# Decay factors and scaled copies of a delta rule moved to ScalarE, a mask moved back, modulation spread over 18 tiles

## The reference

```
proj = h @ w_in;  qkv, z, b_raw, a_raw = split(proj)
qkv  = silu(causal_dwconv(qkv, conv_w))          # 4 taps
q, k = l2_normalize(q) * dk**-0.5, l2_normalize(k)
beta = sigmoid(b_raw);  g = -exp(a_log) * softplus(a_raw + dt_bias)
G    = cumsum(g);  decay = exp(G_i - G_j) for i >= j, else 0
L    = strict_lower((k*beta) @ k.T * decay);  A = L + I
u, w = A^-1 (v*beta),  A^-1 (k*beta*exp(G))
attn = (q @ k.T) * decay
per chunk: v_new = u - w @ S;  o = (q*exp(G)) @ S + attn @ v_new
           S = S*exp(g_last) + (k*exp(g_last - G)).T @ v_new
out  = rms_norm(o) * silu(z) @ w_out
```

## Time and profile before

| | us |
|---|---|
| three runs | 1538.74, 1539.1, 1534.84; median 1538.74 |
| profiled execution | 1539.63, its span 1537.8 |
| busy, TensorE | 1391.5 (90% of the span) |
| busy, VectorE | 851.6 (55%) |
| busy, ScalarE | 533.9 (35%) |
| busy, GpSimd | 171.3 (11%) |
| mean granted clock of TensorE | 0.952 |

### The profile page before, as it was taken

One profiled execution on the slowest core, in us unless ns is written; L12 is line 12 of the kernel. 1 busy time (PEld: TensorE's weight loads), 2 busy tenths in 40 slices (PEclk: granted clock), 3 DMA queues, 4 the chain that ended last, 5 costly groups with the idle time before them and its releaser, 6 DMA issues. The chain is left out here.

```text
span 1537.8 us, 17933 instructions
## 1 busy us (share of the span) xinstructions
PE 1391.5 (90%) x6983; PEld 1121.7 (73%) x6983; DVE 851.6 (55%) x1384; ACT 533.9 (35%) x956; POOL 171.3 (11%) x171
## 2 busy tenths in 40 slices
PE   5798889889879999999998696889989999999997
PEld 5676767779768878887886474646767888888885
DVE  4679899647454654555545538966453323332335
ACT  2353522445342222221223434557343222221321
POOL 0013230004310000000001101220010000000002
PEclk9899999899989999999999798889999999999999
DMA  9443412110404545554532120010102223322321
GB/s 330 142 164 111 162 56 83 56 55 1 164 28 155 201 139 189 185 196 166 167 121 69 33 71 28 28 56 2 55 28 82 82 82 110 110 82 82 110 73 65
DMA packets 102854, 158.36 MB, mean 103 GB/s; under 512 B 9326, under 2 KB 74107, under 8 KB 102779
## 3 DMA queue, kind: packets, MB, share of 16 engines
q1 hardware_dynamic: 91898, 115.40, 22.6%
q0 software_dynamic: 10880, 41.95, 7.8%
HBM read 155.24 MB, written 2.10 MB: 102 GB/s over the span
## 5 line engine op out<-in xcount | busy, mean ns | idle before, releaser
L396 PE MATMUL ps<-h_hi,w_hi 128*128 128x512 f32 x960 | 389.6, 406 | 6.4 <-DVE h_lo L824 6.4
L397 PE MATMUL ps<-h_lo,w_hi 128*128 128x512 f32 x960 | 382.7, 399 | 0.0
L398 PE MATMUL ps<-h_hi,w_lo 128*128 128x512 f32 x960 | 382.2, 398 | 0.0
L380 DVE TENSOR_TENSOR w_lo<-raw,w_hi 128x1024 fp32r<-128x1024 f32 x172 | 210.7, 1231 | 265.9 <-ACT w_hi L374 265.6
L374 ACT ACTIVATE w_hi<-raw 128x1024 fp32r<-128x1024 f32 x180 | 187.9, 1049 | 150.4 <-PE ps L1935 142.9
L396 PEld LDWEIGHTS ps<-h_hi,w_hi 128*128 128x128 f32 x960 | 183.9, 192 | 50.5 <-issue 9.0
L397 PEld LDWEIGHTS ps<-h_lo,w_hi 128*128 128x128 f32 x960 | 184.0, 192 | 43.2 <-issue 1.7
L398 PEld LDWEIGHTS ps<-h_hi,w_lo 128*128 128x128 f32 x960 | 183.2, 191 | 43.6
L448 DVE SCALAR_TENSOR_TENSOR ada_acc<-ada_in,c_act,ada_acc 128x512 f32<-128x512 f32 x147 | 112.8, 768 | 3.9
L1933 PE MATMUL ps<-w_hi,g_hi 128*128 128x512 f32 x256 | 101.6, 397 | 2.6 <-DVE w_lo L380 2.6
L1800 ACT ACTIVATE g_hi<-tmp 128x512 fp32r<-128x512 f32 x44 | 27.8, 632 | 211.9 <-DVE tmp L1835 211.9
(11 more groups left out here) (369 smaller groups left out, 2059.9 us busy)
## 6 DMA issues: line engine op xcount, KB each, us to landing
raw<-in_ffn_w_in_dram SPq DMA_DIRECT2D x44, 1024.0 KB, 5.1
ada_in<-in_ada_w_dram POOLq DMA_DIRECT2D x40, 1024.0 KB, 5.6
raw<-in_ffn_w_out_dram SPq DMA_DIRECT2D x20, 1024.0 KB, 5.0
raw<-in_gdn_w_in_dram SPq DMA_DIRECT2D x16, 1024.0 KB, 5.7
ada_in<-in_ada_w_dram SPq DMA_DIRECT2D x4, 1024.0 KB, 7.3
x_t<-in_x_dram SPq DMA_DIRECT2D x2, 2048.0 KB, 9.8
early_slab<-in_ada_w_dram SPq DMA_DIRECT2D x4, 1024.0 KB, 12.4
raw<-in_gdn_w_out_dram SPq DMA_DIRECT2D x4, 1024.0 KB, 5.0
```

Source lines behind the costliest of these rows:

```text
L380: ops.tensor_tensor(lo, raw_tile(s, kc) if src is None else src, f32(hi), ALU.subtract).then_inc(lo_done, 1)
L396: nc.tensor.matmul(out_, hi[:, k, :], r_hi[:, k, :], start=k == 0, stop=False)
L397: nc.tensor.matmul(out_, hi[:, k, :], r_lo[:, k, :], start=False, stop=False)
L398: last = nc.tensor.matmul(out_, lo[:, k, :], r_hi[:, k, :], start=False, stop=k == kc - 1)
```

## The change

`act_j` takes the place of `pool_j` and `act_eb` that of `pool_eb`, both with four 128x128 instructions per unit in place of one 128x512. `dve_d` is gone: `act_abs` reads the bank of the grow matmul itself, with the negated column sums `g_neg` as its bias, again in four pieces, and stands behind `act_conv_out` in the slot. kk, l, the diagonals, the v turns and va each come one slot later; the elimination is cut into five slots in place of six. `pool_eu` starts when `diagonals` is signalled. The modulation's slabs 4 to 9 take three slots each. In the states, the scaled keys lie in other memory, two small sums come later, and around the last units the late weight splits come ahead of the norm and gate.

```diff
@@ -211,2 +211,3 @@
         gexp = fixed("gexp", [P, 3, NB, H], at=ba_at)
+        g_neg = gdn("g_neg", [P, NB, H])
         k_r = gdn("k_r", [P, NB, H])
@@ -916,3 +917,3 @@
         sq_ring = [diag[:, :, :].rearrange("p a b -> p (a b)"), tmp[:, 2, :]]
-        kg_ring = [diag[:, :, :], tmp[:, 2, :].rearrange("p (h n) -> p h n", h=HG)]
+        kg_ring = [h_raw[:, HG * g:HG * g + HG, (NB - 1) * P:NB * P] for g in range(NG)]
         r_ring = [tmp[:, i, :].rearrange("p (h n) -> p h n", h=HG) for i in range(2)]
@@ -926,4 +927,4 @@
             if TO_GATES <= n < TO_QUERIES:
-                if n == TO_GATES:
-                    act.wait_ge(ada_used, 18)
+                if n % 4 == 0:
+                    act.wait_ge(ada_used, 17 + (n - TO_GATES) // 4)
                 nc.scalar.activation(z_t[:, n - TO_GATES, :], bank, ACT.Silu).then_inc(sem("gdn_out_of_ps"), 1)
@@ -1042,2 +1043,3 @@
                                      ps[:, 6, 0:2 * NB * H].rearrange("p (t a b) -> p t a b", t=2, a=NB)))
+            ch(nc.vector.tensor_scalar(g_neg[:, :, :], gsum[:, 0, :, :], -1.0, None, ALU.mult))
             tt(gsum[:, 2, :, :], gsum[:, 1, :, :], gsum[:, 0, :, :], ALU.subtract).then_inc(sem("g_sums_made"), 1)
@@ -1045,13 +1047,15 @@
 
-        def pool_j(pool, m):
+        def act_j(act, m):
 
             if m == 0:
-                pool.wait_ge(sem("small_made"), 1)
-            nc.gpsimd.tensor_tensor(unit(eu, m), over_heads(upto[:, :]), along(columns(gate, m)),
-                                    ALU.mult).then_inc(sem("j_made"), 1)
+                act.wait_ge(sem("small_made"), 1)
+                act.wait_ge(sem("consts"), 2)
+            for h in range(HG):
+                nc.scalar.activation(eu[:, 4 * m + h, :], upto[:, :], ACT.Identity, scale=column(gate, m, h))\
+                    .then_inc(sem("j_made"), 1)
 
         def pe_grow(pe, m):
-            pe.wait_ge(sem("j_made"), m + 1)
+            pe.wait_ge(sem("j_made"), 4 * m + 4)
             if m >= 2:
-                pe.wait_ge(sem("d_made"), m - 1)
+                pe.wait_ge(sem("abs_made"), 4 * (m - 1))
             nc.tensor.matmul(ps[:, 2 + m % 2, :], ones[:, :], flat(unit(eu, m)), start=True, stop=True)\
@@ -1059,10 +1063,10 @@
 
-        def dve_d(dve, m):
-            dve.wait_ge(sem("grow_mm"), m + 1)
-            tt(unit(eu, m), heads_of(2 + m % 2), along(columns(gsum[:, 0, :, :], m)), ALU.subtract)\
-                .then_inc(sem("d_made"), 1)
-
         def act_abs(act, m):
-            act.wait_ge(sem("d_made"), m + 1)
-            nc.scalar.activation(unit(eu, m), unit(eu, m), ACT.Abs).then_inc(sem("abs_made"), 1)
+
+            if m == 0:
+                act.wait_ge(sem("g_sums_made"), 1)
+            act.wait_ge(sem("grow_mm"), m + 1)
+            for h in range(HG):
+                nc.scalar.activation(eu[:, 4 * m + h, :], heads_of(2 + m % 2)[:, h, :], ACT.Abs,
+                                     bias=column(g_neg, m, h)).then_inc(sem("abs_made"), 1)
 
@@ -1073,3 +1077,3 @@
             for half_ in range(2):
-                act.wait_ge(sem("abs_made"), 4 * half_ + 4)
+                act.wait_ge(sem("abs_made"), 16 * half_ + 16)
                 part = eu[:, 16 * half_:16 * half_ + 16, :]
@@ -1108,12 +1112,13 @@
 
-        def pool_eb(pool, m):
+        def act_eb(act, m):
 
             if m == 0:
-                pool.wait_ge(sem("nb_made"), 1)
-            pool.wait_ge(sem("e_made"), 1 + m // 4)
-            nc.gpsimd.tensor_tensor(unit(lt, m), unit(eu, m), along(columns(nb_f, m)), ALU.mult)\
-                .then_inc(sem("eb_made"), 1)
+                act.wait_ge(sem("nb_made"), 1)
+            act.wait_ge(sem("e_made"), 1 + m // 4)
+            for h in range(HG):
+                nc.scalar.activation(lt[:, 4 * m + h, :], eu[:, 4 * m + h, :], ACT.Identity, scale=column(nb_f, m, h))\
+                    .then_inc(sem("eb_made"), 1)
 
         def pool_eu(pool, m):
-            pool.wait_ge(sem("e_made"), 1 + m // 4)
+            pool.wait_ge(sem("eb_made"), 4 * m + 4)
             nc.gpsimd.tensor_tensor(unit(eu, m), unit(eu, m), over_heads(upto[:, :]), ALU.mult)\
@@ -1127,3 +1132,3 @@
             else:
-                pe.wait_ge(sem("d_made"), 7 + m)
+                pe.wait_ge(sem("abs_made"), 4 * (7 + m))
             k = chunk(H, m)
@@ -1136,3 +1141,3 @@
             dve.wait_ge(sem("kk_mm"), m + 1)
-            dve.wait_ge(sem("eb_made"), m + 1)
+            dve.wait_ge(sem("eb_made"), 4 * m + 4)
             tt(unit(lt, m), heads_of(2 + m % 2), unit(lt, m), ALU.mult).then_inc(sem("l_made"), 1)
@@ -1177,3 +1182,3 @@
 
-            if steps[0] == 1:
+            if 1 in steps:
                 dve.wait_ge(sem("bt_cut"), 2)
@@ -1309,9 +1314,5 @@
 
-            if n < 6 or 8 <= n < 14:
-                j = 4 + n // 3 if n < 6 else 7 + (n - 8) // 3
-                at = n % 3 if n < 6 else (n - 8) % 3
-                out_and(j, ((0, 1), (2,), (3,))[at])
-            elif n < 16:
-                out_and(6 if n < 8 else 9, (0, 1) if n % 2 == 0 else (2, 3))
-            elif n == 17:
+            if n < 18:
+                out_and(4 + n // 3, ((0, 1), (2,), (3,))[n % 3])
+            elif n == 19:
                 dve_ada_out(dve, ch, 9)
@@ -1319,4 +1320,3 @@
 
-        ELIMINATE = {17: range(1, 5), 18: range(5, 9), 19: range(9, 13), 20: range(13, 17), 21: range(17, 24),
-                     22: range(24, 31)}
+        ELIMINATE = {18: range(1, 7), 19: range(7, 12), 20: range(12, 17), 21: range(17, 23), 22: range(23, 31)}
 
@@ -1329,5 +1329,2 @@
                 out_split_act(act, 0, Q_GDN_OUT, n % 4)
-            if 9 <= n < 13:
-                act_abs(act, 2 * (n - 9))
-                act_abs(act, 2 * (n - 9) + 1)
             if not TO_GATES <= n < TO_QUERIES:
@@ -1340,4 +1337,13 @@
                 act_gates(act)
+            if 6 <= n < 10:
+                act_j(act, 2 * (n - 6))
+                act_j(act, 2 * (n - 6) + 1)
+            if 9 <= n < 13:
+                act_abs(act, 2 * (n - 9))
+                act_abs(act, 2 * (n - 9) + 1)
             if n == 12:
                 act_decay(act)
+            if 13 <= n < 17:
+                act_eb(act, 2 * (n - 13))
+                act_eb(act, 2 * (n - 13) + 1)
             if n == 25:
@@ -1378,14 +1384,10 @@
                 dve_g_sums(dve, ch)
-            if 8 <= n < 12:
-                dve.wait_ge(sem("g_sums_made"), 1)
-                dve_d(dve, 2 * (n - 8))
-                dve_d(dve, 2 * (n - 8) + 1)
-            if 13 <= n < 17:
-                dve_l(dve, 2 * (n - 13))
-                dve_l(dve, 2 * (n - 13) + 1)
-            if n == 16:
+            if 14 <= n < 18:
+                dve_l(dve, 2 * (n - 14))
+                dve_l(dve, 2 * (n - 14) + 1)
+            if n == 17:
                 dve_diagonals(dve)
-            if 17 <= n < 21:
-                dve_va(dve, 2 * (n - 17))
-                dve_va(dve, 2 * (n - 17) + 1)
+            if 18 <= n < 22:
+                dve_va(dve, 2 * (n - 18))
+                dve_va(dve, 2 * (n - 18) + 1)
             if n in ELIMINATE:
@@ -1421,4 +1423,4 @@
                 pe_g_sums(pe)
-            if n in (3, 6, 8, 11, 14, 16):
-                pe_ada(pe, {3: 4, 6: 5, 8: 6, 11: 7, 14: 8, 16: 9}[n])
+            if n % 3 == 0 and 3 <= n < 19:
+                pe_ada(pe, 3 + n // 3)
             if 8 <= n < 12:
@@ -1426,8 +1428,8 @@
                 pe_grow(pe, 2 * (n - 8) + 1)
-            if 13 <= n < 17:
-                pe_kk(pe, 2 * (n - 13))
-                pe_kk(pe, 2 * (n - 13) + 1)
-            if 17 <= n < 21:
-                pe_v_turn(pe, 2 * (n - 17))
-                pe_v_turn(pe, 2 * (n - 17) + 1)
+            if 14 <= n < 18:
+                pe_kk(pe, 2 * (n - 14))
+                pe_kk(pe, 2 * (n - 14) + 1)
+            if 18 <= n < 22:
+                pe_v_turn(pe, 2 * (n - 18))
+                pe_v_turn(pe, 2 * (n - 18) + 1)
             if n == 25:
@@ -1453,4 +1455,2 @@
                 gdn_slot_pe(pe, n)
-            pe_sum_of(pe, 14)
-            pe_sum_of(pe, 15)
 
@@ -1461,15 +1461,8 @@
             load_ada(pool, 0, 6)
-            for m in range(4):
-                pool_j(pool, m)
             load_ada(pool, 0, 7)
-            for m in range(4, UNITS):
-                pool_j(pool, m)
             pool_k_root(pool)
             load_ada(pool, 0, 8)
-            for m in range(4):
-                pool_eb(pool, m)
             load_ada(pool, 0, 9)
-            for m in range(4, UNITS):
-                pool_eb(pool, m)
             pool_strict(pool)
+            pool.wait_ge(sem("diagonals"), NB)
             for m in range(UNITS):
@@ -1484,4 +1477,2 @@
             act.wait_ge(sem("kt_mm"), m + 1)
-            if m == 0:
-                act.wait_ge(sem("qk_sum"), 2 * H)
             for h in range(HG):
@@ -1520,7 +1511,6 @@
                     o_rounded(act, m - 2)
-            o_square(act, UNITS - 1)
             for s in range(4):
```

(23 more changed lines are left out.)

## The result

The changed kernel took 1559.61 us, the kernel before beside it 1538.92. That 1559.61 is the median of four executions, one of which was disturbed, at 3237.89 us, and is left out of the ratio; the other three took 1556.85, 1558.62 and 1560.61. The ratio is 1.0132, 95% interval 1.0116 to 1.0147, so the change costs about 20 us. The forecast was 1555, in 1543 to 1566. The profiled execution took 1558.62 us, its span is 1557.0 (1537.8 before), its mean granted clock 0.946 (0.952).

What follows compares the result with a forecast made beforehand. TensorE, nearly always busy, was held by VectorE's late products, VectorE by GpSimd. The terms summed to +16.5 on the profiled 1539.63 us, 1556.1; that execution lay 0.9 over the median, so forecast 1555, range 1543 to 1566.

Steps and rivals of the forecast that it cites:

- (a): Slots 6 to 8: j leaves GpSimd, but TensorE waited for nothing here: 0; tile 9 comes 0.9 us earlier.
- R1: Faster: GpSimd's hold on VectorE makes TensorE wait and ScalarE's abs come in time; sum -7.2, 1531.5 us; chance 0.06.
- (b) to (e): Slots 9 to 17: TensorE waits for ScalarE's abs, last l a slot later; VectorE's four transposes at 229.3, +25.8 us.
- (b): Slot 9: grow(2) waits 11.0 us for a ScalarE chain that begins when tile 9 ends; starts at 142.5, +3.6.
- R2: No change: the new wait takes the old one's place, once; +18.1 shrinks to 3, sum +1.4, 1540 us; chance 0.07.
- R5: Faster than forecast: the masks cost nothing and the small copies are 0.20 us apart, not 0.27; 1547 us; chance 0.10.
- (f): VectorE's work from its transposes to `diagonals`: the elimination loses GpSimd's multiplies beside it; -10.8 us.
- (g): Slot 24: eight GpSimd masks beside three conv steps and a split, one mask per VectorE instruction; +5.1 us.
- R4: The masks starve VectorE, 10.2 us for 5.1, and 3.8 on the transposes; 1564 us; chance 0.15.
- (h): Entry into the states: TensorE's first turn waits as before and the late sums fall into idle time; 0, within 1.
- R3: The clock does not come back between the three grow waits; +10, 1565 us; chance 0.12.
- (i): Exit of the states: late splits go ahead, a 1.95 us wait and some 1.6 of slow matmuls go; -3.6 us.

Runs made afterwards that it cites:

- the chain alone: Kernel before with only the decay factors' step changed: VectorE's subtraction gone, ScalarE's abs reads the grow bank in four pieces with a bias; 1563.15 us, ratio 1.0169.

## Why the prediction was right

The mechanism and its place were as the prediction put them: slower, by a chain through ScalarE that begins only when tile 9, 10 or 11 ends, in a ring of two banks. Up to tile 31 the size was right too. The steps:

- (a) 0 for j. Right for this change (j back on GpSimd: 1559.21 us, ratio 1.0131 for 1.0132), but in part by luck: the reason given was that TensorE waited for nothing in slots 6 to 8. By itself the move is worth 5 to 6 us, since the step that GpSimd holds in slot 7 makes the grow pair of slot 9 late; the new wait there swallows that. Rival R1 saw the lever (GpSimd's hold on VectorE) and had it outweighed, which is what happened.
- (b) to (e): grow(2) at 142.12 for 142.5, T12 at 181.89 for 182.1, T16 at 218.25 for 217.9, the transposes at 229.71 for 229.3. Most terms came from rows of the same shape; two errors in (b) cancel in part, as tile 9 ended at 130.7 for 131.5 and the chain behind it took 11.4 us for 11.0. R2 (the wait is taken once only) was refuted by three waits and by the chain alone, +25. So was R5's half on the small copies, which are 0.26 us apart and not 0.20.
- (f) -10.8, `diagonals` at 282.3: it was 282.61, the products at 0.19 to 0.41 us.
- (g) +5.1: too large, 2.9. One mask per VectorE instruction was read out of the elimination; here four instructions together lost 2.9, of which the split 1.1. R4 is out, and R5's other half, that the masks cost nothing: the transposes took 6.12 us beside the masks and 6.07 without. That is as the Trainium skill ("SBUF — State Buffer", section "SBUF: two separate sides") has it for VectorE instructions with one SBUF input outside the two-port modes.
- (h) 0 within 1: this is the step that was off most: +5.4 to +5.9. The prediction let the late sums fall into idle time and gave the clock no term here. But where before a wait of 3.3 us and small sums stood there is now a wait of 5.23 us, and the clock stayed low for 17 us in this stretch, before for 6.8. R3 had a clock that does not come back as a danger between the grow waits, where tiles of 24 matmuls stand; it came instead among small matmuls at the entry, 180 us later. With the short stretch the same code would have made about 1554, the 1558.62 of the traced execution less 5 (an estimate from the two traces).
- (i) -3.6: alone it measured -3.1. In the changed kernel's trace the same stretch gave back 5.6, in part because late matmuls ran at the full clock where before they did not: 2.05 us for the 16 behind `diag`, before 3.15.

In the trace: +18.8 to tile 31 (20.1 predicted), +5.9 at the entry (0), -5.6 behind it (-3.6): 19.1 for 16.5. At tile 31 the trace is 1.3 under the sum, and the exit gave back 2.0 more than predicted; together they offset more than half of the 5.9 that the entry lacked, so that the sum came so near is in part luck. The terms that missed in size were the masks, and the two places where the clock decides.

## What to carry to other kernels

When a PSUM product's reader moves to another engine, ask what stands ahead of the reader in that engine's order and how many banks the ring has. Here two banks and a reader behind this tile's own copies cost 25 us, and four banks 0, with the same instructions. And when a change helps in one place and makes a new wait behind it, undo the help alone and apply it alone: here j was worth 0 in the changed kernel and 5 to 6 us without it. And one trace per kernel can mislead by 5 us where the clock differs between traces of the same code: look at the granted clock ahead of the order of work.

## What the runs showed of the hardware

- Eight GpSimd multiplies of 128x512 that nobody waits for cost 7.4 us by the medians (1533.16 to 1540.58), 6.8 by the ratios (0.9965 to 1.0009): three VectorE steps that take 2.33 us took 6.56 beside four of them.
- Float32 transposes on VectorE took 6.12 us beside GpSimd's masks and 6.07 without: not held.
- A row of eight 128x128 ScalarE copies with a bias column out of PSUM took 2.13 to 2.16 us, 0.26 apart.
- On the same code, with the same wait of 5.23 us, the 1.2 GHz level lasted 3.6 us beyond the wait in one trace and 16 us in another, among products of 128x128. Each of the fourteen traces has either 6.8 or 17.1 us of it at this place.
